# Forgetting attention: two woven units ahead of the first step in place of four, and ScalarE's mixed tiles one step later

## The reference

```python
def fox_mixer(h, w_qg, w_out, k, v, c):
    ...
    proj = h @ w_qg
    q, g = jnp.split(proj, [D_MODEL], axis=-1)
    q = q.reshape(B, S, H, DH) * (DH ** -0.5)
    ...
    def block(args):
        qi, ci, st = args
        logits = jnp.einsum('bqhd,bkhd->bhqk', qi, k).astype(jnp.float32)
        logits = logits + (ci[..., :, None] - c[..., None, :])
        qpos = st + jnp.arange(BLK)
        mask = key_pos[None, :] <= qpos[:, None]
        logits = jnp.where(mask, logits, -jnp.inf)
        p = jax.nn.softmax(logits, axis=-1)
        return jnp.einsum('bhqk,bkhd->bqhd', p.astype(v.dtype), v)
    ...
    o = o * jax.nn.sigmoid(g)
    return o @ w_out
```

## Time and profile before

| | |
|---|---|
| median of three runs | 2535.69 us |
| profiled execution | 2535.38 us, its span 2533.6 us |
| PE busy | 2467.4 us (97% of the span) |
| DVE, ACT, POOL busy | 1533.9, 1072.7, 90.9 us |
| granted TensorE clock, mean | 0.991 of 2.4 GHz |
| attention steps, first to last scores or values matmul | 749.6 to 913 us |

### The profile page before, as it was taken

One profiled execution on the slowest core, in us unless ns is written; L12 is line 12 of the kernel. 1 busy time (PEld: TensorE's weight loads), 2 busy tenths in 40 slices (PEclk: granted clock), 3 DMA queues, 4 the chain that ended last, 5 costly groups with the idle time before them and its releaser, 6 DMA issues.

```text
span 2533.6 us, 32920 instructions
## 1 busy us (share of the span) xinstructions
PE 2467.4 (97%) x13155; PEld 2001.9 (79%) x13155; DVE 1533.9 (61%) x2579; ACT 1072.7 (42%) x1762; POOL 90.9 (4%) x126
## 2 busy tenths in 40 slices
PE   8998999999999999999998998999999999999999
PEld 7887788887976677888878876888888776888887
DVE  7565766877456647656566355666654897534433
ACT  4544543334335645433345245422323645422323
POOL 2000000100000000000000000011100000000000
PEclk9999999999999999999999999999999999999999
DMA  6333235554222122332324211366642332232331
GB/s 184 107 104 109 83 117 160 172 157 126 77 83 59 51 83 75 100 92 92 91 92 147 84 59 51 123 200 192 191 150 83 92 101 61 89 100 92 100 99 51
DMA packets 286159, 271.16 MB, mean 107 GB/s; under 512 B 11811, under 2 KB 270167, under 8 KB 286007
## 3 DMA queue, kind: packets, MB, share of 16 engines
q1 hardware_dynamic: 267143, 210.33, 27.2%
q0 software_dynamic: 15088, 54.40, 7.3%
q10 hardware_dynamic: 3776, 4.34, 0.6%
HBM read 262.72 MB, written 2.10 MB: 105 GB/s over the span
## 4 chain that ended last, share of the span: by engine, by line
PE 88%; DVE 7%; ACT 3%; issue 1%; DMA 0%; ACTq 0%; DVEq 0%
PE G L2634 69%; PE G L2650 5%; PE G L2589 4%; DVE w_lo L603 1%; PE G L2583 1%; DVE SQ L2387 1%; PE M L1318 1%; PE M L1329 1%; PE M L2167 1%; PE M L1307 1%; PE M L950 1%; ACT w_hi L598 1%; DVE S L2387 1%; PE M L1783 1%; PE M L1794 1%
## 5 line engine op out<-in xcount | busy, mean ns | idle before, releaser
L603 DVE TENSOR_TENSOR w_lo<-raw,w_hi 128x1024 fp32r<-128x1024 f32 x396 | 482.8, 1224 | 637.9 <-ACT w_hi L598 636.8
L2634 PE MATMUL G<-H_hi,w_hi 128*128 128x512 f32 (+1 forms) x1952 | 770.1, 395 | 6.6 <-DVE H_lo L414 2.4
L2634 PE MATMUL G<-H_hi,w_lo 128*128 128x512 f32 (+1 forms) x1952 | 758.4, 389 | 0.0
L2634 PE MATMUL G<-H_lo,w_hi 128*128 128x512 f32 (+1 forms) x1952 | 758.0, 388 | 0.0
L598 ACT ACTIVATE w_hi<-raw 128x1024 fp32r<-128x1024 f32 x396 | 416.7, 1057 | 784.4 <-PE G L2634 704.9
L2634 PEld LDWEIGHTS G<-H_hi,w_hi 128*128 128x128 f32 x1952 | 367.6, 188 | 103.8 <-issue 26.1
L2634 PEld LDWEIGHTS G<-H_hi,w_lo 128*128 128x128 f32 x1952 | 367.2, 188 | 76.2
L2634 PEld LDWEIGHTS G<-H_lo,w_hi 128*128 128x128 f32 x1952 | 367.5, 188 | 72.2 <-issue 0.5
L2634 PE MATMUL G<-hid_hi,w_hi 128*128 128x512 f32 x752 | 294.6, 392 | 2.7 <-DVE Y L754 2.7
L2634 PE MATMUL G<-hid_hi,w_lo 128*128 128x512 f32 x752 | 293.9, 391 | 0.0
L2634 PE MATMUL G<-hid_lo,w_hi 128*128 128x512 f32 x752 | 293.7, 391 | 0.0
(11 more groups left out here) (413 smaller groups left out, 2744.3 us busy)
## 6 DMA issues: line engine op xcount, KB each, us to landing
raw<-in_w_ff SPq DMA_DIRECT2D x128, 512.0 KB
mod_w<-in_w_mod POOLq DMA_DIRECT2D x96, 512.0 KB, 4.4
raw<-in_ffn_w_up SPq DMA_DIRECT2D x176, 256.0 KB
raw<-in_ffn_w_down SPq DMA_DIRECT2D x32, 512.0 KB
raw<-in_w_in SPq DMA_DIRECT2D x28, 512.0 KB
raw<-in_mlstm_w_in SPq DMA_DIRECT2D x24, 512.0 KB
raw<-in_kv_w SPq DMA_DIRECT2D x16, 512.0 KB
raw<-in_fox_w_qg SPq DMA_DIRECT2D x16, 512.0 KB
```

The source lines that it names most:

```text
L603: dve.tensor_tensor(w_lo[:, j, :], raw[:, j, :], w_hi[:, j, :], ALU.subtract).then_inc(lo_done, 1)
L2634: mm = pe.matmul(G[:, 2 * p + m, 0:n], lw[:, k, ms], rh[:, t, 0:n], start=(t == 0 and q == 0), stop=(t == st["ktiles"] - 1 and q == 2), sk ...
```

## The change

Two woven units in place of four stand ahead of step 0, one on each side of the first scores. The woven steps become 27 in place of 26, so step 26 has two units. ACT's table of mixed tiles moves one step on, DVE's table stays.

```diff
-        FOX_AHEAD = 4
+        FOX_AHEAD = 2
         FOX_PAIRS = FOX_HEADS // 2
         FOX_STEPS = TB * FOX_PAIRS
         WOVEN_STEPS = (8 * 7 - FOX_AHEAD) // 2
...
             work = woven()
             next(work)
-            next(work)
             wait_all_read(pe, "kv_k")
             scores(0)
             next(work)
-            next(work)
             outs = linear_units("x_out", H_hi, H_lo, need=from_h("fox"), behind=squares_behind("post1"), every=1)
...
                 if n == WOVEN_STEPS:
                     finish(work)
                     act.wait_ge(chunk_used, used_after("x_g3"))
-                for t in {26: (0, 1), 27: (2, 3), 28: (4,), 29: (5,)}.get(n, ()):
+                for t in {27: (0, 1), 28: (2, 3), 29: (4,), 30: (5,)}.get(n, ()):
                     mixed(t)
```

## The result

| | before | after |
|---|---|---|
| median | 2535.29 us (2533.13 to 2536.72, 5 runs) | 2546.88 us (2546.36 to 2548.21, 5 runs) |
| ratio | 1 | 1.0046 [1.0032, 1.006] |
| profiled execution, span | 2535.38, 2533.6 us | 2546.69, 2544.9 us |

The account below looks back on a forecast made before the run. TensorE bounds the kernel, busy in 97% of the span. From 2535.38 us, -2.74 - 0.1 (front) + 7.2 (stalls) + 2.4 (clock) + 3.9 (end) = +10.7 us gives 2546; range 2540.0 to 2550.5.

Parts of the forecast that it names:

- Front: Ahead of step 0: two units fewer bring scores 2.74 us earlier; two small waits cancel to -0.1 us.
- Stalls: Scores of steps 8, 16 and 24 wait for ACT's late xQ copy: 3 x 2.40 = +7.2 us.
- Rival (c): Cheap end, PE's units lying in the hole and only the stalls left: +4.0 us, 2539.5; chance 0.10.
- rival (e): Nothing measurable: stalls under 2 us and a cheap end cancel, 2533 to 2539 us; chance 0.06.
- Clock: Behind the three xQ gaps PE's clock falls, counted at half the full price: 3 x 0.8 = +2.4 us.
- Rival (a): The three xQ gaps do not pull the clock down: +8.3 us, 2544; chance 0.28.
- Rival (b): Clock falls behind all three gaps, plus another slow stretch in the tail: 2549 to 2550 us; chance 0.14.
- The end, first half: Steps 26 and 27: PE waits some 1.9 us for xPT; first x_out unit at 891.8, +2.3 us.
- The end, second half: From step 28: DVE's H_lo waits for ACT's H_hi, logits queue behind; step 30's transpose at 908.65, end +3.9 us.
- Outside the stage: Everything outside the attention stage's listed terms was put at nothing.
- Rival (d): Hole at 880 to 890 us, step 26, is filled at full clock: -5.5 us, 2530; chance 0.05.
- slower by more: Measured time slower by more than the 0.2%, 5.1 us, that can be told from no change: chance 0.83.

Follow-up runs that it names:

- e1: Changed kernel with ScalarE's and VectorE's read-out of the woven stages one step earlier again, ScalarE's H_hi table still late: 2536.29 us, ratio 1.0007.
- e9: Kernel before, with only ScalarE's and VectorE's read-out of the woven stages one step later, four units ahead and tables as before: 2544.62 us, ratio 1.0038.
- e5: Changed kernel with ScalarE's read-out of a woven stage put ahead of that stage's second weight split: median 2541.0 us of 12 runs, ratio 1.0023.
- e3: Changed kernel with early read-out and the old end both restored, so ScalarE's queue is as before and PE's two units stay moved: 2532.99 us, ratio 0.9994.
- e4: Kernel before, with four units ahead, and ScalarE's H_hi table alone one step later: 2536.77 us, ratio 1.0012.
- e8: Changed kernel with early read-out, put before the second split, and a reordered end with xPT copies ahead of exps in step 27: 2533.05 us, ratio 0.9995.
- e6: Changed kernel with VectorE's H_lo table one step later as well: 2545.94 us, ratio 1.0047.
- e2: Changed kernel with the end (steps, H_hi table, finish) as before and the late xQ read-out kept: 2543.24 us, ratio 1.0036.

## Why the prediction was right, point by point

In what follows a time of the changed kernel less 7.69 us, its lateness at scores(26), is a time on the prediction's old axis.

- **Front.** -2.84 expected (two units, the two small waits), -2.99 measured. The first scores wait 0.19 us where 0.2 was expected, and the 0.28 us wait is gone.
- **Stalls.** 3 x 2.40 expected, 3 x 2.33 of idle and 2.41 of shift measured, at the three places named, released by xQ. e1 takes them away and e9 makes them alone, so this cause is shown. Rival (c), the cheap end with only the stalls left, and rival (e), stalls under 2 us, fall with e1's dear end and the 2.33 us.
- **Clock.** +2.4 expected as half of three falls, +3.15 measured as two of three. This term was right in kind and a little small. Its price of 1.6 us, from the earlier trace rows, was measured as 1.60 and 1.55. That two of three fell and not one is chance as far as the runs show (last section). Rival (a), no fall, holds only for the shorter gaps of e5; the 2.07 us gap that spoke for it has no fall in the kernel before, but in e3, e4, e5 and e8 it has one (clock 0.91 from 1350 to 1370 us). Rival (b), three falls, occurred in none of four kernels with such gaps. The Trainium skill, "TensorE: Matmul & The Clock Gate", section "What's actually happening", has the throttled state as the default and activity as what releases it; the slow rows behind 830.91, which end in the full clock without any change in the work, agree, but which of three equal gaps has its fall that rule does not say.
- **The end, first half.** Scores(27) at 884.23 on the old axis, measured 891.91 - 7.69 = 884.22. First x_out unit at 891.8, measured 891.78. The wait for xPT 1.9, measured 1.82.
- **The end, second half: the term of the sum that was mis-sized.** "PE's transpose of step 30 starts at 908.65": measured 917.60 - 7.69 = 909.91, and the end is +5.16 in place of +3.9, a miss of 1.26. Half of it, 0.60, was there when logits(31) started (914.49 - 7.69 = 906.80 against 906.2): it grew over the steps before, where H_lo tile 4 and logits(30) behind it are 0.64 late, and no single cause of it was sought. The other half comes from "Logits(31) take 1.8 us and the first half of scaled(30) 0.6": it follows PE's wait through DVE alone. These two sizes were right, and scaled(30) ended at 916.86, but PE's transposes came 0.74 us behind it and not 0.05. In the rows the transposes of step 29, one before, wait 1.41 us for a copy that on ACT stands behind the exps of step 31, and those wait for DVE's late logits. The working went through ACT's exps and copies at every step but this last. e4, which has the wait without any moved unit, and e6, where it vanishes, bear this out.
- **Outside the stage** I had counted nothing; the kernel was 0.30 us late ahead of it, and -1.55 us came back behind it. So two misses (+2.0 in the stage, clock and end together, and -1.25 outside it) partly cancel in the total, by luck. The forecast of 2546.0 against 2546.88 looks more exact than its terms were.
- **Rival (d), faster.** Its condition was that the stalls be short. Without any, and with the table as before (e3), the change costs nothing that the runs can tell. But its gain of 5.5 us isn't there. The window 880 to 890 does become full and fast, yet the hole stands behind scores(27) and goes where these go.
- **Chances.** Those for "slower by more" add up to 0.82, not 0.83.

## What to carry to other kernels

When work woven into a loop is taken from its head, look at everything whose place is counted from the units done: a read-out that slips by one step stalls its consumer by what the slip exceeds the time to spare. Here the copy to xQ slipped by 4.5 us (1.85 later by the rows, with PE 2.69 earlier) and had 2.2 us to spare; that is the stall of 2.33 us, at each of the three query stages. The gate stages slipped too, and nobody waited for them. Before matmuls are put "into a hole", find the instruction that starts the chain which makes the hole: work placed ahead of that one pushes the hole along, as in e3. That work placed behind it would fill the hole is to be expected, but no run here tests it. Where one engine writes a tile and another reads it by two hand-made tables, moving one table puts a wait at the head of the reader's queue, and what pays is whatever stands behind it, here at third hand: logits, exps, and a copy that was ready.

## What the runs showed of the hardware

The clock's answer to a gap does not hang on the gap's length alone. Behind PE gaps of 2.33 us in dense work it fell in 8 of 12 cases (the profiles of the changed kernel, e2, e6 and e9, three gaps each), at 1.6 us a fall in the changed kernel; behind those of 1.39 us in none of three (e5). Which of the three it was differs: the second and third in the changed kernel and e6, the first and second in e2 and e9. The changed kernel and e6 run alike to 0.1 us up to there, so these are fewer than twelve independent cases. In the thin work of the end shorter gaps are followed by falls too: in the changed kernel the wait of 1.82 us that ended at 895.23, ahead of the next wait,

```profile
896.50:897.00 0.50, 0.50 (x3) 0.20 (x1) 0.47 (x2) 0.50 (x2) 0.00 (x0) 0.50 0.00 0
```

and of the four waits of 1.41 us (the changed kernel, e1, e4, e5) the one in e1.

That one gap in one and the same code can go either way shows at 260 us, ahead of everything that any edit here touches. PE waits 2.65 or 2.66 us there in all ten profiles. The clock falls behind it in six (before, after, e1, e3, e4, e6) and not in four (e2, e5, e8, e9). The changed kernel and e2:

```profile
260.00:267.00 7.00, 6.43 (x21) 5.04 (x22) 7.00 (x12) 4.96 (x9) 0.00 (x0) 0.76 0.00 0
260.00:267.00 7.00, 6.07 (x25) 4.72 (x26) 7.00 (x12) 4.96 (x9) 0.00 (x0) 1.00 0.00 0
```

A gap of the kernel's later part, alike before and after, shows the same. In the profile before it is 2.69 us and followed by a clock of 0.72; in the profile after, its timeline row and its window:

```profile
1324.29 0.50 PE L2632 MATMUL G<-hid_hi,w_hi 128*128 128x512 f32 x1 [2.70 <-DVE Y L754]
```
```profile
1324.00:1330.00 6.00, 5.71 (x25) 4.70 (x26) 3.73 (x4) 3.06 (x4) 0.00 (x0) 1.00 0.59 190
```

The same wait, the same work behind it, and full speed: the changed kernel gains 1.58 us on the one before here. It loses 1.27 us again behind the gap of 2.26 us at 1520 us (now 1531), where its clock is 0.53 over 11 us against 0.69, and gains 1.62 us at 1927 us (now 1939), where the clock before is 0.72 over 6 us and now 1.00. These three make -1.93, some 0.4 us are lost in small steps around them, and 1.55 us came back. None has a cause in the change that a run shows.

Whether the fall depends on where the gap lies in time, as a cause, no run here tests. So a forecast should count such gaps by a share of falls and not one by one. Executions of one kernel differ in their mean granted clock as such falls would make them: of the 27 runs of the kernel before beside e1 to e4, the 8 with a mean granted clock of 0.991 have a median of 2535.93 us, the 15 with 0.993 one of 2534.03, and the one with 0.995 took 2530.50.
